# Reordering the two layer-norm closes, the early spare weight buffers and the x1 store of a four-layer token model

## The reference, cut to what matters

```python
def layer_norm(x, g, b):
    mu = jnp.mean(xf, -1, keepdims=True)
    var = jnp.mean(jnp.square(xf - mu), -1, keepdims=True)
    return ((xf - mu) * lax.rsqrt(var + LN_EPS) * g + b)
...
for i in range(DEPTH):          # i = 0: ssd_mixer, i = 1: dsa_mixer
    h = mixer(x)                # ends in ... @ w_out, (256 x 4096) @ (4096 x 2048)
    x = layer_norm(DN_ALPHA * x + h, ln_g[i], ln_b[i])
...
hn = rms_norm_2(h, norm_g[0]); proj = hn @ w_in      # third layer, gmlp
```

## Time and profile before

| | |
|---|---|
| median of three runs | 2461.91 us (2460.89 to 2462.85) |
| the profiled execution | 2461.91 us, of which the span is 2460.2 us |
| TensorE busy | 2435.3 us, 99% of the span |
| VectorE, ScalarE, GpSimd busy | 1566.9, 1236.3, 92.9 us |
| granted TensorE clock, mean | 0.998 |
| DMA | 459.53 MB, mean 187 GB/s |

### The profile page before, as it was taken

One profiled execution on the slowest core, in us unless ns is written; L12 is line 12 of the kernel. 1 busy time (PEld: TensorE's weight loads), 2 busy tenths in 40 slices (PEclk: granted clock), 3 DMA queues, 4 the chain that ended last, 5 costly groups with the idle time before them and its releaser, 6 DMA issues.

```text
span 2460.2 us, 45395 instructions
## 1 busy us (share of the span) xinstructions
PE 2435.3 (99%) x19640; PEld 2344.6 (95%) x19640; DVE 1566.9 (64%) x2097; ACT 1236.3 (50%) x1415; POOL 92.9 (4%) x70
## 2 busy tenths in 40 slices
PE   8999999999999999999999999999999999999998
PEld 7999999999999999999988899999999999999998
DVE  5768887866577776665575556656555555555556
ACT  4445666554454565554464445445444445455453
POOL 0001100010022000000000000000000000000002
PEclk9999999999999999999999999999999999999999
DMA  6766666557755655446756666666655565555544
GB/s 178 231 197 187 191 197 189 180 172 234 236 172 175 197 155 163 152 149 235 228 179 188 190 187 194 193 184 190 184 189 189 189 196 172 175 171 170 186 156 172
DMA packets 264840, 459.53 MB, mean 187 GB/s; under 512 B 18667, under 2 KB 69953, under 8 KB 262721
## 3 DMA queue, kind: packets, MB, share of 16 engines
q1 hardware_dynamic: 264641, 456.63, 59.2%
HBM read 452.18 MB, written 4.26 MB: 186 GB/s over the span
## 4 chain that ended last, share of the span: by engine, by line
PE 96%; DVE 1%; DMA 1%; ACT 1%; issue 1%; SPq 0%; POOL 0%; ACTq 0%
PE G L678 89%; PE M L678 5%; PE M L691 1%; DMA WS<-in_a_w_s 0%; DVE W L1494 0%; DMA XS<-in_x 0%; ACT W L1085 0%; DVE BT L1533 0%; DMA RAW<-in_ssd_w_in 0%; DVE WY L1494 0%; DVE W0m L1494 0%; DVE W2m L1494 0%; DVE E L1586 0%; ACT RES L1475 0%; ACT W2m L1085 0%
## 5 line engine op out<-in xcount | busy, mean ns | idle before, releaser
L678 PE MATMUL G<-AA,W 128*128 128x256 f32 x7884 | 942.1, 278 | 5.8 <-DVE W L1494 5.7
L678 PEld LDWEIGHTS G<-AA,W 128*128 128x128 f32 x7884 | 916.9, 188 | 12.7 <-DVE W L1494 6.7
L1494 DVE TENSOR_TENSOR W<-RAW,W 128x1024 fp32r<-128x1024 f32 x431 | 539.3, 1253 | 366.6 <-ACT W L1085 364.9
L1085 ACT CAST W<-RAW 128x1024 fp32r<-128x1024 f32 x431 | 449.0, 1046 | 469.1 <-PE G L678 454.9
L678 PE MATMUL G<-AA,WY 128*128 128x256 f32 x2532 | 308.7, 278 | 0.0
L678 PEld LDWEIGHTS G<-AA,WY 128*128 128x128 f32 x2532 | 296.7, 188 | 2.6 <-issue 2.2
L1494 DVE TENSOR_TENSOR WY<-RAW,WY 128x1024 fp32r<-128x1024 f32 (+1 forms) x127 | 159.3, 1256 | 89.3 <-ACT WY L1085 89.3
L678 PE MATMUL G<-W,AA 128*128 128x512 f32 x864 | 205.7, 394 | 0.0
L678 PEld LDWEIGHTS G<-W,AA 128*128 128x128 f32 x864 | 161.3, 187 | 39.6
L678 PE MATMUL G<-W2m,YY 128*128 128x256 f32 x1536 | 186.6, 276 | 1.0 <-DVE W2m L1494 1.0
L678 PE MATMUL G<-W1m,YY 128*128 128x256 f32 x1536 | 185.7, 276 | 0.1
(11 more groups left out here) (289 smaller groups left out, 2338.2 us busy)
## 6 DMA issues: line engine op xcount, KB each, us to landing
RAW<-in_a_w_in SPq DMA_DIRECT2D x192, 512.0 KB, 3.7
RAW<-in_ssd_w_in SPq DMA_DIRECT2D x160, 512.0 KB, 4.4
RAW<-in_b_w_in SPq DMA_DIRECT2D x128, 512.0 KB, 4.0
RAW<-in_dsa_w_in SPq DMA_DIRECT2D x72, 512.0 KB, 3.5
RAW<-in_ssd_w_out SPq DMA_DIRECT2D x64, 512.0 KB, 4.8
RAW<-in_dsa_w_out SPq DMA_DIRECT2D x64, 512.0 KB, 4.2
RAW<-in_a_w_out SPq DMA_DIRECT2D x64, 512.0 KB, 3.5
RAW<-in_b_w_out SPq DMA_DIRECT2D x32, 512.0 KB, 3.8
```

The costliest lines, as they stand in the source:

```text
L678: return e.matmul(o, l, r, start=start, stop=stop, skip_group_check=True)
L1085: e.copy(wh[:, 0:n], RAW[:, v % NR, 0:n]).then_inc(*up(cast_done, "cast", v))
L1494: e.tensor_tensor(wl[:, 0:n], RAW[:, v % NR, 0:n], wh[:, 0:n].bitcast(F), ALU.subtract).then_inc(*up(rest_done, "rest", v))
```

## The change

It changes five things. (1) The ten spare slots: all five a open at one unit, o1 block 1 index 9, and all five b at o2 block 1 index 7, instead of one by one over the following units. (2) `ln_open` issues its four residual loads at once. (3) `ln_close`: on DVE the reciprocal follows the moments directly, `tails(0,1)` is ahead of `close(1)`, and `gain(1,0)` and `tails(1,0)` have two `normal` operations between them; on ACT `gain(0,2)` is ahead of `root(1)`; on PE the fourth group's transposes, (1,0), and all behind them come one unit later. (4) The normed rows: for s = 1 POOL makes all 16 operations in a row as soon as `at1(3,1)` is there; for s = 2 POOL makes the eight of half 0 in the same way and DVE only the eight of half 1, with ACT's squares of half 1 two ticks earlier and DVE's sum one tick earlier. (5) `x1_store` comes in SP's queue at the end of block ms, directly behind `ev_ms`.

```diff
--- before.py
+++ after.py
@@ -134,9 +134,9 @@
         extra = {"y1": (first["bc", 1], last["z", 7] + 1), "z1": (first["bc", 1], last["z", 6] + 1),
                  "y3": (first["ms", 0], last["gate", 7] + 1), "y5": (first["v5", 0], last["z5", 6] + 1),
                  "x7": (first["k7", 0], last["z7", 3] + 1)}
-        for i, (j, n) in enumerate(((1, 12), (2, 1), (2, 6), (2, 11), (3, 2))):
-            extra[f"a{i}"] = (self.blocks["o1", j][n], first["ms", 0])
-            extra[f"b{i}"] = (self.blocks["o2", j][n], first["v5", 1])
+        for i in range(5):
+            extra[f"a{i}"] = (self.blocks["o1", 1][9], first["ms", 0])
+            extra[f"b{i}"] = (self.blocks["o2", 1][7], first["v5", 1])
         free = [(i, None) for i in range(3)]
         self.slot, self.prior, self.turn = {}, {}, {}
         self.slot_end, ready = {}, 0
@@ -461,13 +461,13 @@
         start("set3")
         start("ev_cq")
         tick()
-        run(("ms", 0), ("ev_ms",))
+        run(("ms", 0), ("ev_ms",), ("x1_store",))
         run(("gate", 0), ("ev_gate", 0))
         for i in range(2):
             run(("qi", i), ("ev_qi", i))
         start("index")
         for j in range(8):
-            run(("q", j), ("ev_q", j), *((("x1_store",),) if j == 1 else ()))
+            run(("q", j), ("ev_q", j))
             run(("k", j), ("ev_k", j))
             n = (15, 3, 0, 0, 0, 0, 0, 4)[j]
             run(("v", j), ("ev_v", j), later(n, "attend", j, 0), later(n, "attend", j, 1), later(n + 8, "gated", j))
@@ -631,8 +631,7 @@
             for i in range(4):
                 e.dma_start(to[:, :, 512 * i:512 * i + 512], src[:, :, 512 * i:512 * i + 512]).then_inc(
                     *landed(res_here[i], "res", s, i))
-                for _ in range(4):
-                    yield
+            yield
 
         def ln_rows(s):
             e.wait_ge(*on("unit", plan.blocks["o1" if s == 1 else "o2", 4][3]))
@@ -861,7 +861,7 @@
                 last.then_inc(*up(pe_made, "xt_t2", s, h, g))
                 yield
             if s == 2:
-                for _ in range(10):
+                for _ in range(9):
                     yield
                 turn_scale("r5")
                 yield
@@ -1205,8 +1205,8 @@
             gain(0, 1)
             top(0, 1)
             yield
+            gain(0, 2)
             root(1)
-            gain(0, 2)
             top(0, 2)
             yield
             top(1, 0)
@@ -1222,16 +1222,13 @@
                     yield
                 e.wait_ge(*done(("v5", 0)))
                 for t in range(2):
-                    if t:
-                        yield
-                        yield
-                        yield
                     for q in range(2):
                         e.wait_ge(*on("x2", t))
                         if t or q:
                             e.wait_ge(*on("r5_s", t, q - 1) if q else on("r5_s", t - 1, 1))
                         e.activation(SQUARES["r5"], RES4[:, t, 1024 * q:1024 * q + 1024], ACT.Square,
                                      accum_out=SQS[:, t, q:q + 1]).then_inc(*up(act_made, "r5_s", t, q))
+                    yield
                 e.wait_ge(*on("r5", "sum"))
                 e.activation(CC[:, 0:2], CC[:, 0:2], ACT.Sqrt, scale=1.0 / DM, bias=eps6[:, 0:1]).then_inc(
                     *up(act_made, "r5", "root"))
@@ -1698,8 +1695,6 @@
                 e.wait_ge(*on("st", s, 4, h))
                 e.bn_aggr(MV[:, h, :], ST[:, h, :, :].rearrange("p a b -> p (a b)")).then_inc(
                     *up(dve_made, "mv", s, h))
-
-            def spread(h):
                 e.wait_ge(*on("sd", s, h))
                 e.reciprocal(RSD[:, h:h + 1], RSD[:, h:h + 1]).then_inc(*up(dve_made, "rsd", s, h))
 
@@ -1728,7 +1723,6 @@
                     *up(dve_made, f"at{s}", g, h))
 
             close(0)
-            spread(0)
             normal(0, 0)
             normal(0, 1)
             gain(0, 0)
@@ -1736,16 +1730,15 @@
             normal(0, 3)
             yield
             tails(0, 0)
+            tails(0, 1)
             close(1)
-            tails(0, 1)
-            spread(1)
             normal(1, 0)
             normal(1, 1)
+            tails(0, 2)
+            gain(1, 0)
             normal(1, 2)
-            gain(1, 0)
-            tails(0, 2)
+            normal(1, 3)
             tails(1, 0)
-            normal(1, 3)
             yield
             tails(1, 1)
             yield
@@ -1755,9 +1748,12 @@
             if s == 2:
                 for _ in range(6):
                     yield
-                for n in range(8):
-                    gained(n // 4, n % 4)
+                for g in range(4):
+                    gained(1, g)
                     yield
+                yield
+                yield
+                yield
                 e.wait_ge(*on("r5_s", 1, 1))
                 e.tensor_reduce(CC[:, 0:2], SQS[:, :, 0:2], AX.X, ALU.add).then_inc(*up(dve_made, "r5", "sum"))
                 e.wait_ge(*on("r5", "root"))
@@ -2275,20 +2271,18 @@
 
         def ln_close(s):
 
-            if s == 2:
-                return
-            e.wait_ge(*on("gains", s))
-            us = plan.blocks["ms", 0] + plan.blocks["gate", 0]
-            for t in range(2):
+            yield
+            for t in range(3 - s):
+                e.wait_ge(*on("gains", s))
+                e.wait_ge(*on(f"at{s}", 3, 1))
                 for g in range(4):
                     c = slice(512 * g, 512 * g + 512)
-                    e.wait_ge(*on("unit", us.pop(0)))
-                    e.tensor_tensor(XH[:, t, c], XH[:, t, c], ROWS[:, 0, c], ALU.mult).then_inc(
+                    to = (XH, RES4)[s - 1][:, t, c]
+                    e.tensor_tensor(to, XH[:, t, c], ROWS[:, 0, c], ALU.mult).then_inc(
                         *up(pool_made, "x_g", s, t, g))
-                    e.wait_ge(*on("unit", us.pop(0)))
                     e.wait_ge(*on("x_g", s, t, g))
-                    e.tensor_tensor(XH[:, t, c], XH[:, t, c], ROWS[:, 1, c], ALU.add).then_inc(
-                        *up(pool_made, "y1", t))
+                    e.tensor_tensor(to, to, ROWS[:, 1, c], ALU.add).then_inc(
+                        *up(pool_made, *(("y1", t) if s == 1 else ("x2", t))))
             yield
 
         def set3():
```

## The result

| | before | after |
|---|---|---|
| median, same chip, four runs each | 2461.40 us (2460.64 to 2462.85) | 2476.44 us (2475.50 to 2480.07) |
| ratio after to before, 95% interval | | 1.0076 (1.0063 to 1.0088) |
| profiled execution, and its span | 2461.91, 2460.2 us | 2482.3, 2481.0 us |

The change makes the kernel slower. The ratio rests on all seventeen executions of the changed kernel (2475.5 to 2483.8 us, the middle one at 2480.7), so it says more than the four-run median: 0.0076 x 2461 = 18.7 us, by its interval 15.5 to 21.7. The profiled execution lies 2482.3 - 2461.91 = 20.4 us above that of before. The direction was as forecast and the size was not: 8.9 us were forecast.

The account below looks back on a forecast made before the run. PE's own work was taken to bound the kernel, with no wait to remove near the change. Stalls of 1.55 + 0 + 1.2 + 1.55 + 4.6 = 8.9 us on 2461.91 gave 2470.8 us, range 2464 to 2480.

Parts of the forecast that it names:

- The step that failed: Spare slots and residual loads: earlier slots can't hurt PE, as units are still cast in PE's order; cost 0.
- The margin of 6.5 us: Weight load behind the residual: of 13.6 us until PE needs it, 6.5 are left after landing, cast and rest.
- the tight place: Block ms under POOL's first-layer burst: DVE just holds PE's pace, margin shrinks to about 0.5 us, cost 0.
- its upper end of 2 us: Block ms: the other end of the cost of 0, given two more turns of POOL.
- The closes: Both closes: the new order stalls PE 1.55 us at each; 1.2 to 2.0 for the first.
- the named place: First unit of each half-1 pass: PE waits about 1.5 us on `tails` (AA, L1498).
- The third layer's start: Behind the second close, POOL and DVE taking turns: PE stalls 2.4 and 0.9 on rests, 1.3 later; together 4.6 us.
- The third, 1.3 on Z: Third layer's start: PE waits for transposes' input near 1290, ready 1291.3, wanted 1290.0; stall 1.3 us.
- The store: Behind block ms: issued about 741.3, landed 10.1 us later, delaying weight loads; PE stalls 1.2 us, 0 to 4.
- The rival that the clock falls as well: One to three clock falls behind the forecast stalls add 1.8 to 5.4 us: 2472.6 to 2476.2; beyond 2476: 0.22.

Follow-up runs that it names:

- f4: The whole change, with DVE's `ln_block` of blocks 0 and 1 of both output products written four units earlier: 2469.09 us, ratio 1.0035 to the kernel before.
- e4: The kernel before with only the five slots opened at once and the four residual loads at once: 2472.90 us, ratio 1.0043.
- e1: The changed kernel with spare slots opened one by one and residual loads four ticks apart, as before: 2466.57 us, ratio 1.0027 to the kernel before.
- e5: The kernel before with only the new order inside both closes (`ln_close` on PE, ACT and DVE): 2463.11 us, ratio 1.0011.
- e6: The kernel before with only the s = 2 normed rows split, POOL half 0 and DVE half 1: 2463.88 us, ratio 1.0014.
- e8: The kernel before with POOL's 16 operations of s = 1 in a row and the store moved behind block ms: 2460.30 us, ratio 1.0000.
- e7: The kernel before with POOL's 16 operations of s = 1 in a row, the store at its old place: 2460.10 us, ratio 0.9998.
- f3: The kernel before with residual loads at once and only two of five slots opened at once, three staggered: 2461.70 us, ratio 1.0002.
- e2: The changed kernel with spare slots opened one by one, the four residual loads still at once: 2466.63 us, ratio 1.0026 to the kernel before.
- e3: The changed kernel with residual loads four ticks apart again, the five slots still at once: 2473.40 us, ratio 1.0056 to the kernel before.

## Why the prediction was wrong

The parts by effect, in us, with what the profile of the changed kernel shows for each:

| part | forecast | measured | from |
|---|---|---|---|
| 1 and 2 on DVE's order | 0 | 10.1 | change less f4; e4 alone 10.6; profile 5.2 + 7.1 |
| 1 with 4 or 3, block ms | 0 (0 to 2) | 2.0 | f4 less e1; profile: idle 1.29, 2.1 in all |
| 3, both closes | 3.1 | 2.7 | e5; profile: 2 waits of 1.14 |
| 4, s = 2 | 4.6 | 3.4 | e6; profile: waits of 2.18 and 1.47, 4.2 in all |
| 5, the store | 1.2 | 0 | e8 |
| sum | 8.9 | 18.2 | the change: 18.7 |

Each measured effect has an interval of two to four us either way, so it is partly luck that the sum meets the 18.7 so closely.

**The step that failed** is the first one of its working: "More slots earlier can't hurt PE by themselves, since units are still cast in PE's order." It asked whether the weights would be there in time for PE, and they were. It did not ask what else DVE has in its queue. With more slots open, `walk` writes the rests of units further ahead, and every other DVE instruction of that stretch then stands behind rests that wait for loads. The margin of 6.5 us worked out for a weight load was of no use, since the stall is on RES. The earlier trace rows had nothing on it either: a list of waits can't show a margin. What would have shown it is the timeline of before at 598 to 603 us: a margin of 3.2 us, less than three rests of 1.23, on a line that the change doesn't touch but puts four rests ahead of.

**Block ms** was named as the tight place, and its upper end of 2 us is what was measured, but for a reason that the working lacked. It took POOL's turns and PE's own lateness as the only changes there. With POOL alone (e7) they cost nothing, as forecast; in the changed kernel the cast comes 11 us later as well, of which some 7 are PE's own lateness, and the margin is gone.

**The closes** came as worked out: 1.4 us each for the 1.55 forecast, with the wait at the named place. **The third layer's start** too: two waits on rests, 2.18 and 1.47 us, against the 2.4 and 0.9 forecast, and a stand of ACT of 6.72 us. The third, 1.3 on Z, is missing in the changed kernel and 0.7 in e6. Altogether this start costs 4.2 us in the changed kernel, where 4.6 were forecast. A turn of POOL cost a DVE operation 1.67 - 0.68 = 0.99 or 2.28 - 1.22 = 1.06 us there, and 2.06 - 0.96 = 1.10 in block ms, where 1.10 had been taken from the earlier trace rows. The rule of the Trainium skill (SBUF — State Buffer, Who interferes with whom) would have let a turn cost up to 1.31; that the two engines take turns is what the trace shows, and the smaller figure from the rows was the right one. **The store** was mis-sized by its landing: 8.7 us in the changed kernel and 8.3 in e8 for the 10.1 forecast, and in e8 it was issued at 738.31, where the forecast, less the 1.55 us by which PE was to be late, had 739.8. PE never waited there.

**The rival that the clock falls as well** was right in kind. Its 2472.6 to 2476.2 us, with 2480 as its upper end, lie nearer to what was measured, but by luck: it counted on a fallen clock behind waits that did not lower it in the changed kernel, and knew nothing of the stall that did. Behind the RES waits the granted clock is 0.50 to 0.54, the level of 1.2 GHz, and they lose 1.75 and about 2.7 us more. Behind the waits that had been forecast it stayed at 1.00 in the changed kernel.

What stays open: why the executions of the changed kernel lie up to 8 us apart and those of e4 up to 10. Loads that land at different times, and a fall of the clock that comes or doesn't, would do it; no run here tells the two apart.

## What to carry to other kernels

Before letting an engine run further ahead, list what else is in its queue in that stretch, and for each such instruction who waits for it, and with how much slack against the work that will stand ahead of it; a prefetch can cost time though nobody needs what it fetches. Write short work that frees a resource (here the addition that gives PSUM banks back) ahead of prefetch work that can stall. And where buffers are dealt out in turn, opening them at other moments changes which buffer every later unit gets, so look at the tight places far behind the change as well.

## What the runs showed of the hardware

Whether a wait lowers TensorE's clock isn't decided by its length alone. In the changed kernel a wait of 2.18 us at 1293.93 was followed by 12 matmuls in 3.06 us at clock 1.00. In f4 a wait of 2.17 us at the same place was followed by this (timeline, then a window):

```profile
1280.00 10.37 PE L683 MATMUL G<-W,AA 128*128 128x512 f32 x36 [2.17 <-DVE W L1497]
```

```profile
1282.00:1284.00 2.00, 2.00 (x6) 1.54 (x6) 2.00 (x2) 1.14 (x2) 0.77 (x1) 0.50 0.52 196
```

36 matmuls in 10.37 us, where the earlier trace rows has 8.56, so 1.8 us lost, about what the fall of the earlier trace rows lost behind 2.29 us. At 65 to 66 us, e6 waited 1.99 us and then took 7.41 us for 48 matmuls (at the pitch of 2.72 they take 5.6), and f3 waited 2.23 us and took 3.04 us for 24, the usual time. The plainest case is the wait of the earlier trace rows, 2.29 us in every one of the fourteen profiles: the unit behind it took 3.02 to 3.04 us in six of them (the changed kernel, e2, e3, e5, e6, f3) and 4.22 to 4.63 us in the other eight. The five waits of 2.76 us and more in the profiles of the changed kernel, e3 and e4 were all followed by the lower level. A forecast has to price waits of some 2 us with both outcomes.

A fallen clock isn't always lost time, either. The changed kernel kept its clock behind the 2.18 us and then waited 1.47 us more for the next rest; f4 and e3 went on at the lower level (36 matmuls in 10.37 and 10.38 us) and had no second wait. All three were 4.2 us later than before at the end of it. In the same way the six kernels that kept their clock at 52 us waited 1.9 to 2.2 us at 66 us, and the other eight 0.3 to 0.7 us. Where PE is about to wait for the same operand anyway, the slower units only fill the wait.
